# The expert layer of a two-block model: tokens sorted by expert count instead of by group

## The reference

```python
def _hmoe(h, w_rg, b_rg, w_re, b_re, w_gate, w_up, w_down):
    t = h.reshape(B * S, D)                                   # 256 x 1024
    g_logits = t @ w_rg + b_rg                                # 4 groups
    g_idx = argmax(g_logits); g_w = softmax(g_logits)[g_idx]
    e_logits = (t @ w_re + b_re).reshape(-1, 4, 4)
    e_sel = e_logits[g_idx]                                   # the 4 experts of the group
    top_v, top_i = lax.top_k(e_sel, 2)
    top_w = softmax(top_v) * g_w
    gate = ...                                                # 256 x 16, two entries per token
    y = 0
    for e in range(16):
        he = silu(t @ w_gate[e]) * (t @ w_up[e])              # 1024 -> 512
        y = y + gate[:, e:e + 1] * (he @ w_down[e])           # 512 -> 1024
    return y
```

## Time and profile before

| what | value |
|---|---|
| median of 3 runs | 2254.27 us (2253.61 to 2255.11) |
| the profiled execution, its own time | 2254.26 us |
| its span, first to last instruction | 2252.4 us |
| mean granted TensorE clock over the span | 0.98 of full |
| busy: PE, DVE, ACT | 96%, 70%, 53% of the span |
| DMA over the span | 432.14 MB, mean 192 GB/s |
| expert layer, first wide matmul to last residual add | about 234 to 594 us of the span |

### The profile page before, as it was taken

How to read it: one execution, slowest core, us unless ns; L and a number is a source line. 1 busy time by engine, 2 the same in 40 slices (tenths; PEclk the granted TensorE clock), 3 DMA queues, 4 the chain that set the end, 5 groups by cost and what they waited for, 6 DMA issues and landing times.

```text
span 2252.4 us, 39311 instructions
## 1 busy us (share of the span) xinstructions
PE 2154.1 (96%) x17046; PEld 2041.8 (91%) x17046; DVE 1570.3 (70%) x1942; ACT 1184.1 (53%) x1392; POOL 0.2 (0%) x4
## 2 busy tenths in 40 slices
PE   6978999999899999999998999799999999998997
PEld 5868888888799999999998999799999999998997
DVE  8976899999696677445666774695776545757764
ACT  3554577777453644435855444453654436854442
POOL 0000000000000000000000000000000000000000
PEclk9998999999999999999999999899999999999999
DMA  8473699999354544444343444354544444344542
GB/s 347 171 272 118 244 372 374 370 373 372 140 183 148 192 150 169 150 150 150 113 152 130 172 180 155 131 175 154 198 154 170 164 151 150 113 173 145 188 178 85
DMA packets 64317, 432.14 MB, mean 192 GB/s; under 512 B 7792, under 2 KB 11024, under 8 KB 13712
## 3 DMA queue, kind: packets, MB, share of 16 engines
q1 hardware_dynamic: 64144, 429.61, 52.5%
HBM read 428.50 MB, written 1.08 MB: 191 GB/s over the span
## 4 chain that ended last, share of the span: by engine, by line
PE 88%; DVE 6%; ACT 3%; issue 1%; DMA 1%; SPq 0%; ACTq 0%; DVEq 0%
PE banks L1861 62%; PE banks L1879 10%; PE quad L1879 5%; DVE slot_rounded L997 1%; ACT area_y_rounded L650 1%; DVE area_y L2357 1%; PE quad L552 1%; PE quad L452 1%; PE quad L500 1%; PE single L565 1%; PE quad L516 1%; DVE slot_rounded L2391 1%; PE single L1562 1%; PE quad L472 0%; DVE area_y L1293 0%
## 5 line engine op out<-in xcount | busy, mean ns | idle before, releaser
L1861 PE MATMUL banks<-spare_rounded,slot_rounded 128*128 128x272 f32 (+1 forms) x2176 | 623.8, 287 | 0.0
L1861 PE MATMUL banks<-spare_rounded,area_y_rounded 128*128 128x272 f32 (+1 forms) x1504 | 437.6, 291 | 14.9 <-DVE hn_rounded L986 12.9
L1861 PE MATMUL banks<-area_x_rounded,slot_rounded 128*128 128x272 f32 (+1 forms) x1568 | 447.0, 285 | 0.0
L1861 PE MATMUL banks<-hn_rounded,area_y_rounded 128*128 128x272 f32 (+1 forms) x1504 | 430.9, 287 | 0.0
L1861 PEld LDWEIGHTS banks<-spare_rounded,slot_rounded 128*128 128x128 f32 x2176 | 412.1, 189 | 0.0
L997 DVE TENSOR_TENSOR slot_rounded<-slot,area_y_rounded 128x2048 fp32r<-128x2048 f32 x118 | 269.5, 2290 | 159.7 <-ACT area_y_rounded L650 159.6
L1861 PEld LDWEIGHTS banks<-spare_rounded,area_y_rounded 128*128 128x128 f32 x1504 | 285.3, 190 | 16.7 <-DVE hn_rounded L986 13.8
L1861 PEld LDWEIGHTS banks<-area_x_rounded,slot_rounded 128*128 128x128 f32 x1568 | 296.7, 189 | 0.0
L1861 PEld LDWEIGHTS banks<-hn_rounded,area_y_rounded 128*128 128x128 f32 x1504 | 285.0, 189 | 0.1
L650 ACT ACTIVATE area_y_rounded<-slot 128x2048 fp32r<-128x2048 f32 x118 | 223.7, 1906 | 31.8 <-PE banks L1861 31.8
L997 DVE TENSOR_TENSOR slot_rounded<-slot,area_x_rounded 128x2048 fp32r<-128x2048 f32 x52 | 119.0, 2292 | 91.0 <-ACT area_x_rounded L650 90.8
(11 more groups left out here) (553 smaller groups left out, 5046.4 us busy)
## 6 DMA issues: line engine op xcount, KB each, us to landing
slot<-in_units_second SPq DMA_DIRECT2D x236, 1024.0 KB, 4.8
slot<-in_units_moe SPq DMA_DIRECT2D x100, 1024.0 KB, 4.9
slot<-in_units_first SPq DMA_DIRECT2D x32, 1024.0 KB, 6.1
spare<-in_units_moe SPq DMA_DIRECT2D x20, 1024.0 KB, 5.1
spare<-in_units_first SPq DMA_DIRECT2D x6, 1024.0 KB, 5.2
slot<-in_units_second SPq DMA_DIRECT2D x8, 768.0 KB, 4.2
merged<-acs_rows SPq DMA_DIRECT2D x4, 544.0 KB, 5.0
slot<-in_units_first SPq DMA_DIRECT2D x2, 576.0 KB, 3.9
```

Of the source, the lines that this page charges most:

```text
L1861: ins = nc.tensor.matmul(out, weights[w], x[a], start=start and i == 0, stop=stop and i == 2, **kw)
```

## The change

The tokens are sorted by expert, not by group, and the experts are ranked by their token count on the chip (`count_key`, `rank`, `order`).

- The three largest experts ("natural") take all 256 tokens in their own order, as two row sets of 128, in split form: 72 matmuls for each set.
- The next five ("single") get a block of 128 places each, in split form: 72 matmuls.
- The eight smallest get 64 places each. Two of them share a block ("pair"): each multiplies its 64 places, as 64 stationary columns, by its own weights into one half of the output's partitions. These matmuls are plain f32, unsplit: 16 for gate, 16 for up, 16 for down.

So there are 12 items (3 natural, 4 pairs, 5 singles) with 15 row sets, in the order N0 P0 N1 P1 N2 P2 S0 P3 S1 S2 S3 S4. The work of the PE queue is a list of 45 "blocks of work": two wide ones (gate, up) for each row set, with `down` of the row set two before behind every second one. The loads are 96 units in that order, 12 for a pair and 6 for others, and SP reads each expert's index into a register first; none is issued before the order is known. Ten buffers (two more after the naturals) stand for both raw and high parts: a unit that is rounded holds two of them, one of a pair holds one. 48 units are rounded instead of 120.

Gathers become 24, each of four matmuls of 384 columns that add high and low up; a single's block is split again by `x_high` and `x_low`. Scatters come one row set at a time (11 of them) into three free banks and `single`. The naturals' results are added up in SBUF by DVE (`add_natural`).

```diff
-BLOCKS = N_GROUPS + 1
+NATURALS, SINGLES, PAIRS = 3, 5, 4
+BLOCKS = PAIRS + SINGLES
 class MoePlan:
+        self.items = [natural[0], pair[0], natural[1], pair[1], natural[2], pair[2], single[0], pair[3], *single[1:]]
...
+        for k in range(len(self.wides)):
+            self.blocks.append(("wide", k))
+            if k >= 4 and k % 2 == 0:
+                self.blocks.append(("down", (k - 4) // 2))
...
+        for j in range(len(self.blocks)):
+            due = sum(len(units) for units in rounds[:j + 2]) + (1 if j + 2 < len(rounds) and rounds[j + 2] else 0)
+            self.rounded_by.append(self.rounded[done:due])
...
+        free = [(0, place) for place in range(BUFFERS)]
+        for u in self.units:
+            free.sort()
+            u.raw_after, u.raw = free.pop(0)
+            if u.rounding is not None:
+                u.high_after, u.high = free.pop(0)
+                free.append((u.freed, u.high))
+            free.append((u.freed, u.raw))
...
+BUFFERS = 10
 def expert_sync(...):
+    sp.wait_ge(s.order_known.sem, 1)
+    for u in moe.units:
+        if u.rank not in first_unit:
+            first_unit[u.rank] = sp.value_load(m.order[0:1, u.rank:u.rank + 1], min_val=0, max_val=6 * (EXPERTS - 1))
+        if u.raw_after:
+            sp.wait_ge(s.gemm_moe.sem, s.gemm_moe.at(0, u.raw_after))
+        sp.dma_start(m.moe_plain[u.raw], src).then_inc(m.landed_moe[u.raw].sem, 16)
 # routing, DVE (link: the next one waits for it)
+    link(stt(m.count_key, m.single[:, 96:112], float(EXPERTS), m.minus_expert, ALU.mult, ALU.add))
+    link(tt(m.greater, over_middle(m.count_key), over_last(m.count_key), ALU.is_gt))     # 128 x 16 x 16
+    link(red(m.rank, m.greater, AX_X, ALU.add))
+    link(tt(m.of_rank, over_middle(m.rank), over_last(m.expert_index), ALU.is_equal))
+    link(tt(m.greater, m.of_rank, over_middle(m.unit_of), ALU.mult))
+    link(red(m.order_real, m.greater, AX_X, ALU.add))
+    tick(copy(m.order, m.order_real), s.order_known)
...
 # gathers, PE
+    pe.wait_ge(s.h2_low.sem, 2)
     for n in range(GATHERS):
+        for part in range(2):
             for b in range(2):
+                ins = nc.tensor.matmul(m.gather_bank(n)[:, 0:CHUNK], (m.h2t_high, m.h2t_low)[part][:, b, ...],
+                                       m.place[:, b, CHUNK * chunk:CHUNK * chunk + CHUNK], start=..., stop=...)
 # a pair's gate or up, PE
+        for half in range(2):
+            for u in item.halves[kind][half]:
+                landed(u)
+            for k in range(4):
+                for i, u in enumerate(item.halves[kind][half]):
+                    ins = nc.tensor.matmul(out[64 * i:64 * i + 64, :], m.x_plain(item.block)[:, 4 * half + k, 64 * i:64 * i + 64],
+                                           m.moe_plain[u.raw][:, 512 * k:512 * k + 512], ...)
 # order of PE's list
+    for k, (item, kind, halves) in enumerate(moe.wides):
+        wide_natural / wide_single / wide_pair
+        if k == 0:
+            slot_gates()
+        if k >= 3 and k % 2:
+            if k >= 5:
+                scatter_whole(moe.slots[(k - 5) // 2]) if k < len(moe.wides) - 1 else None
+            turn_into_y(moe.slots[(k - 3) // 2])
+        elif k >= 4:
+            down(moe.slots[(k - 4) // 2])
 # order of ACT's and DVE's lists: for each block of work first the roundings due, then the rest
+    for j, (what, n) in enumerate(moe.blocks):
+        for u in moe.rounded_by[j]:
+            moe_high(act, ...)   /   moe_low(v, ...)
+        ...                       # x_high / x_low, tanh / product, hidden, turned, add_natural, y_high / y_low
+        if 1 <= j <= 3:
+            turn_places(range(3 * j - 3, 3 * j))        # DVE: 3 blocks, two operations of 128 x 256 each
```

More of the change, by code:

```diff
@@ L1417, with __init__ @@
+class Slots:
+    def __init__(self, index, item, b):
+        self.index, self.item, self.b = index, item, b
+        self.scatter = None
 class MoePlan:
     def __init__(self):
[L1421 to L1437, removed]
+        natural = [Item("natural", r, [r], None) for r in range(NATURALS)]
+        pair = [Item("pair", q, [NATURALS + SINGLES + 2 * q, NATURALS + SINGLES + 2 * q + 1], q) for q in range(PAIRS)]
@@ new lines, in __init__ @@
+        used, ticks, self.units = [], 0, []
+        for what, n in self.blocks:
+            item, kind, halves = self.wides[n] if what == "wide" else (self.slots[n].item, "down", (0, 1))
+            units = [u for half in halves for u in item.halves[kind][half]]
+            used.append([u for u in units if u not in self.units])
+            self.units += used[-1]
+            if what == "wide" or self.slots[n] is item.slots[-1]:
+                for u in units:
+                    ticks += 1
+                    u.freed = ticks
@@ new lines, in __init__, with singles @@
+        self.landings = {}
+        for u in self.units:
+            self.landings[u.raw] = self.landings.get(u.raw, 0) + 1
+            u.landing = self.landings[u.raw]
+        for item in self.items:
+            for kind in ("gate", "up", "down"):
+                item.last = {**(item.last if kind != "gate" else {}), kind: item.halves[kind][1][-1]}
+    @property
+    def singles(self):
+        return sorted((item for item in self.items if item.form == "single"), key=lambda item: item.number)
@@ new lines, in naturals_done, with item_of, done @@
+    @property
+    def naturals_done(self):
+        return next(item for item in self.items if item.form == "natural" and item.number == NATURALS - 1).last["up"].freed
+    def item_of(self, unit):
+        return next(item for item in self.items if unit.rank in item.ranks)
+    def done(self, s, x, kind):
+        if x.item.form == "natural" and x.b == 0:
+            return s.moe_side, s.moe_side.at(0, 3 * x.item.number + 1 + ("gate", "up", "down").index(kind))
+        return s.gemm_moe, s.gemm_moe.at(0, x.item.last[kind].freed)
@@ L1862, in split_product @@
     return ins
+GATHER_ON_ACT = [n % 3 != 2 for n in range(GATHERS)]
 def gathered_wait(eng, s):
@@ L1871, in expert_tensor, with low_ready @@
 def expert_tensor(pe, nc, m, s, moe):
[L1873 to L1879, removed]
-        return ins
[L1882 to L1887, removed]
+    def low_ready(u):
+        pe.wait_ge(s.moe_low.sem, s.moe_low.at(0, u.rounding + 1))
@@ L1913, in down @@
         for half in range(2):
-            n = moe.at[p, "down", half]
-            low_ready(n)
-            high, low = weights(n)
+            u = item.halves["down"][half][0]
+            low_ready(u)
             for k in range(2):
                 for cols in range(2):
-                    at = 1024 * k + 512 * cols
-                    ins = product(m.y_slots(block)[:, 512 * cols:512 * cols + 512], [part[:, 2 * half + k, :] for part in (m.hid_high, m.hid_low)],
-                                  (high[:, at:at + 512], low[:, at:at + 512]), e + half + k == 0, e == 3 and half * k == 1)
```

749 lines of the change are left out of this document (503 added, 246 removed).

## The result

The changed kernel took 2231.17 us (median of 4, 2229.60 to 2232.28) against 2253.95 beside it: a ratio of 0.9898, interval 0.9880 to 0.9915, 22.8 us less. The forecast was 2223 in a range of 2204 to 2256. The profiled execution took 2230.94 us; its last residual add ends at 569.09 + 0.87 = 569.96 us (forecast 562.8, before 593.9). Behind that add lie 1659.1 us of span, before 1658.5, so nearly the whole difference is made ahead of it.

A forecast was written before the change was run, and what follows sets the result against it. The prediction took PE to bound the expert layer, with loads and DVE right behind. Start 248, PE's list 297.8 and waits 17.0 gave 562.8 for the last add, 31.1 less than before: 2223 us, range 2204 to 2256.

The forecast's parts named there:

- The step of two halves: Pairs' matmuls on PE: two half-width f32 matmuls side by side take 0.88 us, 96 steps 84.5 us.
- the quarters: Earlier trace's four f32 matmuls into 32 output partitions each, together 0.88 us; taken as the price of two halves.
- the rival of halves one after the other: Pairs on PE: halves don't run side by side, a step is 1.76 us, total about 2300 us; chance 0.06.
- the late start of the loads: Loads wait for the expert order, starting at 224.3 us; costs nothing, as the gathers are later by some 19 us.
- The first wide matmul: Start of PE's expert matmuls, after routing and gathers: about 248 us, 13.5 later than before, bounds 245 to 251.
- the sum: Whole expert layer: start 248, PE's list 297.8 and waits 17.0 give the last add's end at 562.8 us.
- Changes of width: PE's 24 changes between whole and half-width matmuls: put at nothing; 3.7 us if each lost 0.155.
- Scatters: PE's scatter matmuls at 0.125 us: nine scatters of 16 take 18.0 us, two natural ones 2.2.
- Late loads in the naturals: Natural 1: late loads and a rounding ahead of `hidden` on DVE make PE wait 1 us.
- The tight spot: Single 0 with pair 3: thirteen loads, then roundings ahead of pair 2's low copy; PE waits 6.3 us, range 3 to 8.
- Singles: DVE's 18.3 us per single expert barely covered by PE's time; waits of 1 us in all.
- The end: After the last `down`: copies, a scatter and 3.5 us of adds, about 3.5 us beyond PE's list.

The follow-up runs named there:

- e7: Changed kernel with all eight matmuls of a pair's first expert in a block of work, then all eight of the second: 2276.43 us.
- e6: Changed kernel with experts taken in a fixed order, so that loads need not wait for the order: 2230.32 us.
- the repeat: The changed kernel run once more, unaltered, beside later versions on one chip: 2232.82 us.
- e3: Changed kernel where, as a rule, ACT and DVE put roundings due two blocks later behind the block's own steps: 2222.33 us.
- e8: Changed kernel with a small matmul ahead of each pair step but a block's first: whole width 2264.58 us, as two halves 2238.10 us.
- e5: Changed kernel with the pairs' loads bringing half their bytes, which the matmuls read twice: 2220.22 us.
- e1: Changed kernel with the pairs' loops swapped: one expert's matmuls in a half of the weights, then the other's: 2249.64 us.

## Why the prediction was right, and where it was off

The mechanism held. The step of two halves was taken as 0.88 from the quarters and is 0.86; the rival of halves one after the other fell, and e7 shows that it was no empty one. That the late start of the loads costs nothing held (e6). PE stays the bound, with single places where it waits.

The first wide matmul is at 249.8 for 248, and at 246.3 in the repeat; that the sum lies between them is in part luck. Routing starts 1.6 us later than taken (215.67 for 214.06); the granted clock from 140 to 180 us is 0.79 there and 0.87 in the kernel before, but it doesn't order the starts (e3: 0.83 and 211.69; e8 with halves: 0.87 and 214.22). From there to the first gather it took 13.7 us for the 14.0 of the sum, where the DVE steps over 128 x 256, unseen before, took 0.42 to 0.57 us each for the 0.42 assumed. The gathers took 20.4 for 19.9.

The failed step is a size: PE's list and its waits, 569.96 for 562.8 at the last add. From the first wide matmul to the first `turn` it took 32.9 us, where the sum had 27.0 for matmuls and gate weights and 5.2 for waits and the low clock. From there to the end the sum leaves 282.6, and 287.3 were measured. The terms, by their rows:

- Changes of width: put at nothing, from the row that seemed to show no gap; that was the wrong reading. They are 20, not 24, as three pair blocks stand next to each other, and cost 2.7 us: ten times 0.15, six times 0.09 behind whole matmuls and four times 0.17 behind transposes. The alternative that the prediction had worked out from the earlier trace rows, 0.155 for each change, was near (0.135).
- Whole matmuls and transposes: 169.0 us in place of 166.1, 2.9 more; the pace is 0.232 for 0.229. Pairs: 96 x 0.86 = 82.6 for 84.5, 2 less.
- Scatters: 1.74 for each of the two natural ones, where 1.1 was taken for half the width, 1.3 more; the other seven ahead of the last `down` 1.91 for 2.0, 0.6 less.
- Late loads in the naturals: 1 us taken for natural 1, 2.4 measured; a rounding queued ahead of `hidden` holds it up. (The same at natural 0, 1.15, lies ahead of the first turn.) The last `turn` waits for 0.2.
- The tight spot: 6.3 taken, all of it as waits. The mechanism was the one forecast, roundings ahead of the low copy; by e5 the place cost 6.6 and 0.9 behind it, 1.1 more than taken, of which 4.2 and 0.5 are waits and most of the rest is the lower clock behind them.
- Singles: 1 us taken, no wait seen.
- The end: the sum had two scatters and 3.5 us behind the last `down`, 7.5; the last add ends 5.8 behind it, 1.7 less, as the first of the two scatters runs under the copies for the second.

These come to 4.3 of the 4.7 us. Another 0.6 us lies in the second block. Read by starts and not by a modelled end, the change in the earlier trace rows shows a loss too. PE's timeline of the kernel before, from three windows that cut off ever more of the same group:

```profile
25.28 0.34 PE L1562 MATMUL quad<-slot,work 128*32 128x64 f32 x8
25.34 0.28 PE L1562 MATMUL quad<-slot,work 128*32 128x64 f32 x4
25.39 0.23 PE L1562 MATMUL quad<-slot,work 128*32 128x64 f32 x2
```

The quarters follow one another by 0.06 us for four, but the first whole matmul, at 25.60, starts 0.21 behind the last two; unless something else held it, 0.15 us was lost there.

Of the signs that the prediction named, a pair's gate takes 7.0 us (283.24 to 290.26), a single's 19.1 to the next, and the DMA share is 0.79; the last add at 570 in place of 563 missed. The stated range, up to 2256, also held no change at all, so that the number lies in it says little. The sum put at nothing what DVE and ACT no longer have to do, and no run tests that by itself; but the order in which they do the rest was worth 7.1 us (e3), more than any single wait of the sum.

## What to carry to other kernels

Two plain f32 matmuls of half the columns shared the engine here if they stood within two places of each other in the list; write the loop over the halves innermost. When a load is late, look at what is queued behind the engine that waits for it: moving the steps whose inputs are ready ahead of that wait gave 7.1 us (e3), where halving the pairs' bytes gave 8.9 (e5), without making a load any faster. Read the cost of a change in a list from start to start, not from a modelled end. Compare kernels over a stretch that begins behind code they share, when that code's time differs from execution to execution.

## What the runs showed of the hardware

- PE started matmuls of the other half of the output's partitions while two plain f32 matmuls of 512 columns of the first half were still to finish, and not earlier (e1: 285.29, ahead of an earlier one in the list at 286.15; e7: 303.71 and 490.23).
- The two changes between whole and half width around a block of long matmuls cost 0.24 to 0.32 us, and those around one small matmul 0.39 (e8).
- The unchanged attention stage started the routing at 211.6 to 215.7 us in different executions; between the two profiles of the changed kernel (215.67 and 212.39) the granted clock from 140 to 180 us was 0.79 and 0.87, but in e3 it was 0.83 with a start at 211.69.
